# Token halves at the ends of the feed-forwards: a tail of five tiles, and the next norm's transposes among other products

## What is computed

```python
x = x + (gelu(gate) * (h @ ffn_w_val)) @ ffn_w_down      # block 1, gate = causal conv of h @ ffn_w_gate
x = rmsnorm(x, norm_final)
for l in range(2):                                       # block 2
    x = layer_norm(alpha * x + 0.5 * swiglu(x, w_gu[l,0], w_down[l,0]), ...)
    x = layer_norm(alpha * x + token_mixers(x), ...)
    x = layer_norm(alpha * x + 0.5 * swiglu(x, w_gu[l,1], w_down[l,1]), ...)
```

## Time and profile before

| | |
|---|---|
| median of three runs | 1370.58 us |
| profiled execution, span from first to last instruction | 1368.9 us |
| TensorE busy | 1331.6 us, 97% |
| VectorE busy | 893.2 us, 65% |
| ScalarE busy | 755.2 us, 55% |
| chain that ended last | TensorE 77%, VectorE 12%, ScalarE 8% |
| DMA | 228.9 MB, mean 167 GB/s |

### The profile page before, as it was taken

The page is one execution under the profiler, slowest core; times in us unless marked ns, Lnnn a source line. Parts: engine busy times, 40 slices in busy tenths (PEclk is TensorE's granted clock), DMA queues, the critical chain, the costliest instruction groups (busy, mean ns, idle before and its releaser), DMA issues.

```text
span 1368.9 us, 20197 instructions
## 1 busy us (share of the span) xinstructions
PE 1331.6 (97%) x8028; PEld 1154.7 (84%) x8047; DVE 893.2 (65%) x1329; ACT 755.2 (55%) x1216; POOL 80.5 (6%) x132
## 2 busy tenths in 40 slices
PE   7999899999999999999999999999999999999997
PEld 6888788887888889887888888888889887888886
DVE  5887776766665667465766656656667465766565
ACT  6776655555555554655555554655554655555553
POOL 2121000000000002400000000000001500000000
PEclk9999999999999999999999999999999999999999
DMA  7334576664766654333576665766655333476660
GB/s 234 124 124 145 157 223 197 197 209 128 244 187 186 194 163 143 93 124 94 153 241 194 185 186 151 224 195 191 192 155 147 107 124 93 128 235 196 196 196 34
DMA packets 294959, 228.90 MB, mean 167 GB/s; under 512 B 13248, under 2 KB 271443, under 8 KB 294867
## 3 DMA queue, kind: packets, MB, share of 16 engines
q1 hardware_dynamic: 294850, 227.62, 55.0%
q10 hardware_dynamic: 16, 0.00, 0.0%
HBM read 226.54 MB, written 1.05 MB: 166 GB/s over the span
## 4 chain that ended last, share of the span: by engine, by line
PE 77%; DVE 12%; ACT 8%; issue 2%; DMA 2%; POOL 0%; SPq 0%; DVEq 0%; ACTq 0%
PE bank L885 21%; PE bank L802 12%; PE bank L803 12%; PE bank L804 12%; PE bank L888 11%; DVE lo_gu L1763 4%; ACT hi_gu L1369 3%; PE bank L1272 3%; DVE lo_dn L1768 2%; PE bank L1241 2%; DVE conv L1947 1%; DMA st_dn<-in_ffn_w_down 1%; PE bank L1252 1%; ACT conv L1485 1%; DVE xT L1778 1%
## 5 line engine op out<-in xcount | busy, mean ns | idle before, releaser
L885 PE MATMUL bank<-xT,hi_gu 128*128 128x512 f32 x1616 | 404.1, 392 | 2.3 <-DVE lo_gu L1763 2.1
L1763 DVE TENSOR_TENSOR lo_gu<-st_gu,hi_gu 128x2048 fp32r<-128x2048 f32 (+1 forms) x145 | 322.7, 2229 | 101.0 <-ACT hi_gu L1369 101.0
L885 PEld LDWEIGHTS bank<-xT,hi_gu 128*128 128x128 f32 x1616 | 296.7, 189 | 60.7 <-DVE lo_gu L1763 3.3
L1369 ACT ACTIVATE hi_gu<-st_gu 128x2048 fp32r<-128x2048 f32 (+2 forms) x146 | 269.9, 1854 | 0.9 <-DMA st_gu<-in_w_in 0.8
L888 PEld LDWEIGHTS bank<-xT,lo_gu 128*128 128x128 f32 x1616 | 220.8, 191 | 15.9
L888 PE MATMUL bank<-xT,lo_gu 128*128 128x256 f32 x1616 | 225.5, 282 | 0.0
L802 PE MATMUL bank<-hi_dn,actTh 128*128 128x512 f32 x436 | 172.3, 395 | 3.2 <-DVE actTl L1959 3.2
L803 PE MATMUL bank<-lo_dn,actTh 128*128 128x512 f32 x436 | 170.7, 392 | 0.0
L804 PE MATMUL bank<-hi_dn,actTl 128*128 128x512 f32 x436 | 169.9, 390 | 0.0
L1950 DVE TENSOR_TENSOR act<-act,bank 128x256 f32<-128x256 f32 x101 | 42.5, 421 | 177.7 <-ACT act L1492 177.7
L1376 ACT ACTIVATE hi_dn<-st_dn 128x1024 fp32r<-128x1024 f32 x109 | 114.1, 1056 | 62.3 <-DMA st_dn<-in_ffn_w_down 62.3
(11 more groups left out here) (294 smaller groups left out, 1781.5 us busy)
## 6 DMA issues: line engine op xcount, KB each, us to landing
st_gu<-in_ffn_w_gu SPq DMA_DIRECT2D x176, 512.0 KB, 5.1
st_dn<-in_ffn_w_down SPq DMA_DIRECT2D x109, 512.0 KB, 6.3
st_gu<-in_w_in SPq DMA_DIRECT2D x23, 1024.0 KB, 5.4
st_gu<-in_w_out SPq DMA_DIRECT2D x24, 512.0 KB, 4.2
st_gu<-in_ffn_w_gate SPq DMA_DIRECT2D x21, 512.0 KB, 4.2
st_gu<-in_ffn_w_val SPq DMA_DIRECT2D x21, 512.0 KB, 5.6
st_gu<-in_w_in SPq DMA_DIRECT2D x10, 512.0 KB, 4.1
gb<-in_ln_g SPq DMA_DIRECT2D x6, 512.0 KB, 7.0
```

The lines of the kernel that those rows point to most:

```text
L885: pe.matmul(b[:, :], hv[:, w, k, :], xT[:, k, :, :].rearrange("p a b -> p (a b)"), start=k == 0, stop=k == KD - 1, skip_group_check=True)
L1369: i = act.activation(high, staged, ACT.Copy)
L1763: i = dve.tensor_tensor(low, staged, high.bitcast(F32), ALU.subtract)
```

## The change

`TAIL` and `RING` go from 4 to 5: the last five tiles' downs go by token halves, and there is a fifth buffer for down weights, laid over `gbo`. `turn` of the next norm's first token half moves from the start of the next stage to before the last down of the second half (not at norms 4, 7 and 8). `turn` of the second half moves, in feed-forwards 1 to 4, from between the tiles into the first half's products of the second tile (before step k = 6 of 8 in f = 1, 3, before k = 4 in f = 2, 4), and the four fills behind it go. At the start of f = 1, 3 and of the projections two fills stay of four. In VectorE's `norm` the low copies of the first half, and before them at norms 2 and 5 the low weights of the next feed-forward's second tile, come before the second half's add.

```diff
-TAIL = 4
-RING = 4
+TAIL = 5
+RING = 5
...
-            def gate_up_tokens(f, j, m, event=None, turned=None):
+            def gate_up_tokens(f, j, m, event=None, turned=None, norm_turned=None):
...
+                    if norm_turned is not None and k == (KD - 2 if f % 2 else KD // 2):
+                        turn(x, norm_turned, 1)
                     i = mm3(o, (xTh[:, k, ts], xTl[:, k, ts]), (hv[:, :, k, :], lv[:, :, k, :]), k == 0, k == KD - 1)
...
-            def ffn(f, i, src):
+            def ffn(f, i, src, turned_next=None):
+
                 tail = range(FFN_TILES[f] - TAIL, FFN_TILES[f])
-                turn(src, i, 0)
-
                 idle = 6 + tile_no(f, 0) % 2
-                fill(idle, 4)
+                if f % 2:
+                    fill(idle, 2)
+                else:
+                    turn(src, i, 0)
+                    fill(idle, 4)
...
                     gate_up_tokens(f, 0, 0, i)
-                    gate_up_tokens(f, 1, 0)
+                    gate_up_tokens(f, 1, 0, norm_turned=i)
                     fill(idle, 1)
-                    turn(src, i, 1)
-                    fill(idle, 4)
                     gate_up_tokens(f, 0, 1, i)
...
                 for m in range(M):
                     for j in tail:
+                        if m == 1 and j == tail[-1] and turned_next is not None:
+                            turn(x, turned_next, 0)
                         down(f, j, m)
...
-                turn(x, i, 0)
-                fill(7, 4)
+                fill(7, 2)
                 token_half(c, 0, bank[0][:, 0:WCOLS], i)
...
+                    if m == 1 and i != LAST:
+                        if i in (2, 5):
+                            weights_low(CHUNK_NO["ffn", i // 2 + i % 2, 1])
+                        turned_low(i, 0)
                     for h in range(2):
                         add(i, m, h)
                     centre(i, m)
-                    if m == 1 and i != LAST:
-                        turned_low(i, 0)
-                        if i in (2, 5):
-                            weights_low(CHUNK_NO["ffn", i // 2 + i % 2, 1])
                     normalize(i, m)
```

More of the change, by code:

```diff
@@ L268, in program @@
         hi_out2, lo_out2 = over("hi_out2", KD * WCOLS, at_proj), over("lo_out2", KD * WCOLS, at_proj + 4 * KD * WCOLS)
-        hi_dn = [over(f"hi_dn{i}", D, (at_down, at_proj)[i // 2] + 4 * D * (i % 2)) for i in range(RING)]
-        lo_dn = [over(f"lo_dn{i}", D, (at_down, at_proj)[i // 2] + 4 * (KD * WCOLS + D * (i % 2))) for i in range(RING)]
         act32 = sb("act32", [P, 2, S])
@@ L288, in program @@
         rs = sb("rs", [P, M])
+        at_gbo = -(-nc.sbuf_base // 32) * 32
         gbo = sb("gbo", [P, M, D])
+        hi_dn = [over(f"hi_dn{i}", D, (at_down, at_proj)[i // 2] + 4 * D * (i % 2)) for i in range(4)] + [over("hi_dn4", D, at_gbo)]
+        lo_dn = [over(f"lo_dn{i}", D, (at_down, at_proj)[i // 2] + 4 * (KD * WCOLS + D * (i % 2))) for i in range(4)] + [over("lo_dn4", D, at_gbo + 4 * D)]
         ones = sb("ones", [P, 1])
@@ L1107, in tensor_program @@
                     out_part(m, h, 1)
-            ffn(0, 1, n)
+            ffn(0, 1, n, 2)
             def first_projections(l):
@@ L1354, in tensor_program @@
             for l in range(LAYERS):
-                ffn(1 + 2 * l, 2 + 3 * l, x)
+                ffn(1 + 2 * l, 2 + 3 * l, x, 3 + 3 * l)
                 mixers(l)
-                ffn(2 + 2 * l, 4 + 3 * l, x)
+                ffn(2 + 2 * l, 4 + 3 * l, x, 5 + 3 * l if l + 1 < LAYERS else None)
         def scalar_program(act):
```

## The result

The changed kernel takes **1375.7 us** (median of seven runs, 1372.83 to 1377.91) against 1370.58 (seven runs, 1369.91 to 1373.05). The ratio is 1.0035, 95% interval 1.0025 to 1.0044: 5 us slower, where the forecast was no visible change. The profiled execution took 1376.42 us, its span is 1374.9, 6.0 above the one before. Lines on TensorE are one higher than before (L885 is L886), on VectorE and ScalarE five (L1763 is L1768).

A forecast was written before the change was run, and what follows sets the result against it. TensorE, busy 97% of the span, was taken as the bound, except at feed-forward 0's end (vector/scalar loop). Terms 0, +0.3, -0.3, -0.9, +0.6, -0.3, +0.2 gave -0.4 us: 1370.2 us from 1370.58, range 1366.8 to 1372.8.

The forecast's parts named there:

- tail waits: Last gate-up of feed-forwards 1 to 4 waits for its low weights: 0.3, 0.9, 0.55 and 0.2 us.
- joint 2 to 3: From feed-forward 2 into 3: first product no earlier or later, second transposes inside the second tile win 0.9 us.
- 7.4 us chain: Feed-forward ends: vector/scalar loop steps from ScalarE's copy of the down weights to the low weights add up to 7.4 us.
- A deeper ring at no cost: Fifth down-weight buffer over gbo: loosens ScalarE's wait for old downs, which shows in no row; 0 us.
- if the clock stays up: End of feed-forward 0: gate-up 20 waits 1.1 us, keeps full pace, ends at 317.6; last down +1.1 us.
- +2.8 from 319.3: End of feed-forward 0, the other case: gate-up 20 slow again, ends at 319.3; last down 2.8 us later.
- rival B: Tail waits lower the clock for the last gate-ups of feed-forwards 1 to 4: 1377.6 us, 1374 in two; chance 7%.
- Norm 3: Into the first projections: product 0.8 us earlier, but second transposes wait for the late second half; +0.3 us left.
- norm 6: Into the second projections: product earlier, second transposes wait; +0.6 us with the 0.55 us tail wait before it.
- rival A: Handovers and second tiles gain without new waits: 6.9 us, 1363.7 us, half of it 1367; chance 15%.
- no gain and no loss: Into feed-forward 3: first half normed 845.1, low weights and copy until 848.2, so first product at 848.25 as before.
- own case: Whole kernel: no visible change, 1370.2 us, chance 77%; terms' ends -1.2 to +1.3 us, range 1368.5 to 1372.

The follow-up runs named there:

- early down loads: Changed kernel with the last two tiles' loads ordered gate-up pair, down weights, pair, down weights, instead of two pairs then two downs: 1372.7 us, ratio 1.0013.
- The second execution: The changed kernel as it is, run and profiled again beside the other kernels on one chip: 1375.2 us, ratio 1.0036.
- the one that wins: Kernel before with only the second transposes moved inside the second tile: 1369.4 us; with k = 6 in all four feed-forwards 1368.5 us.

## Why the prediction was wrong

The profile came out 6.4 us above the forecast of its change (+6.0 against -0.4). Of these 3.2 are two falls of the clock in the mixers, which the sum did not have; 1.9 are the tail waits beyond their forecast; 0.9 the loops of 1 to 4; 0.5 the joint 2 to 3 beside its wait. The smaller terms add 0.5, and 0.55 had been won by the last tiles of feed-forward 0's loop, before anything that the change moves. In the medians, which are 5.5 us above the forecast, the lower clock has a smaller part (1 to 2 us by the estimate above), and the tail waits are the largest step that an experiment shows.

**Tail waits, feed-forwards 1 to 4: mis-sized.** Forecast 0.3 + 0.9 + 0.55 + 0.2 = 1.95 us; measured from gate-up 20 to 21, beyond 5.59: 0.87 + 0.95 + 1.77 + 0.25 = 3.8. The mechanism and the 7.4 us chain were right. Two things were not. I took the moments at which the down weights had landed from one execution and let them stand, though the change itself may shift the traffic around them: ScalarE's wait at the end of feed-forward 3 went from 1.52 to 2.69 us. And the same kernel has other ones in its next execution: at the end of feed-forward 4 it was 1.11 us in one and 2.04 in the other, and TensorE's wait behind it 0.09 and 0.95. Second, a wait costs more than its bracket, 0.16 us more by the matmuls that no longer overlap, so that the 0.09 us ones lengthen the step by 0.25; and 0.1 more in the gate-up behind it, which the sum of 3.8 leaves out. The early down loads show it: the waits fall to 0.09, and the time by 3.0 us. That is more than the 1.9 that was mis-sized, since it takes away most of the 1.95 that was forecast too.

**A deeper ring at no cost: failed.** I set the fifth buffer at 0. In every kernel with `RING` 5, the one with `TAIL` 4 among them, each fifth tile of the loops is 0.05 us longer and the next 0.02 to 0.03; in none with `RING` 4. Timeline of TensorE in the changed kernel, the 12 downs of tile 24 in buffer five: 371.62 to 374.41 is 2.79 us; the next tile's, 380.00 to 382.74, 2.74.

```profile
371.62 0.39 PE L803 MATMUL bank<-hi_dn,actTh 128*128 128x512 f32 x1
...
374.41 0.39 PE L886 MATMUL bank<-xT,hi_gu 128*128 128x512 f32 x1
...
380.00 0.40 PE L803 MATMUL bank<-hi_dn,actTh 128*128 128x512 f32 x1
...
382.74 0.39 PE L886 MATMUL bank<-xT,hi_gu 128*128 128x512 f32 x1
```

Over the loops of 1 to 4 that is the +0.9 us of the table (0.23 + 0.29 + 0.15 + 0.20). Why these matmuls are slower is open: no run has the fifth buffer at another place.

**Feed-forward 0, "if the clock stays up": right in the profile after, unsafe as a choice.** The case "+2.8 from 319.3" happened in two of the six profiles with five tiles there (the two without the moves), and once the fall came at gate-up 20 with the moves on top (+0.8). The sum took the good case at full weight. One of the last two gate-ups of feed-forward 0 was slow in each of the six profiles with five tiles, never both: in three it was 19, behind 2.08 to 2.16 us; in the other three 19 kept its pace behind 2.16 to 2.18, and 20 was slow behind 2.47 or 2.48. None was slow behind the waits of 0.09 to 1.61 us in 1 to 4. So rival B did not happen, though its 1374 lay near the result.

The case that "TensorE: Matmul & The Clock Gate" of the Trainium skill describes in its section "HAM oscillation — how this bites in real kernels" is one of DMA waits of 3 to 5 us, each longer than any wait here. The prediction put it to waits of 0.2 to 2.3 us, which the section does not do. The traces agree with neither reading: half clock came behind 2.1 us, but not every time.

**The norms and the second tiles: right but for one overlap.** Norm 3 cost 1.08 us and 0.87 of it is the tail wait; norm 6 1.96, of which 1.77: 0.2 us beside the wait, forecast 0 to 0.05. The product came first (520.84 against 520.55 forecast) and the wait went ahead of the second transposes, which rival A excluded. Feed-forwards 2 and 4 started 0.4 us better each (forecast 0.3), with idles of 0.52 and 0.51. Feed-forward 1 starts unchanged (forecast 0). The joint 2 to 3 won 0.3 instead of 0.9. There the forecast let the tail wait of 0.9 us vanish, because VectorE's own chain was to hold the first product back: "no gain and no loss". But VectorE had to wait 0.99 us for the delayed downs of the first half (the row at 842.51), and the first product came 0.5 us later against the tiles before it. With the wait gone the joint won 1.0. The end of feed-forward 4 cost 0.5 (forecast 0.2), 0.36 of it the step and the gate-up behind its wait of 0.09 us.

**The mixers: missing.** Two falls of the clock; the mixers with the first products behind them took 1.6 us more each (from 0.77 late behind norm 3 to 2.39 late at the start of feed-forward 2). They are why the span is 6.0 longer and not some 3. The second execution had none, and its span was as long: it was 1.1 us late at the start of feed-forward 0 already, lost 0.8 where gate-up 20 was slow, and waited longer at the end of feed-forward 4. The range written for the own case, 1368.5 to 1372, is wider than its terms (-1.2 to +1.3 from 1370.2 is 1369.0 to 1371.5), and the result lies outside both. The prediction's last sentence, that a wait ahead of these second transposes decides between it and rival A, held.

What stays open: by medians the changed kernel with early down loads is 2.1 us above the kernel before. Its profile is 3.4 us longer. Of these 1.2 were lost by tile 17 of feed-forward 0, which is the execution and not the kernel: at this tile six profiles of kernels with the same instructions up to there lie from 0.86 ahead to 1.29 behind. Another 1.6 are a fall in the mixers. The remaining 0.6 belong to the kernel (the loops and the four last gate-ups, +1.8, less what the transposes inside and norm 5 win). By the clock of its runs the lower clock costs it about 1 us more than the kernel before (4.7 against 3.7 on average); whether the change brings that about is not shown.

## What to carry to other kernels

Where work is moved from between two products to behind them, the products' next input must be ready earlier by as much: look up which wait already stands behind a DMA on the engine that makes it, and put the load first in its queue; this was worth 3.0 us here. A time at which a DMA lands can be another one in the next execution of the same kernel, so bound it by the longest wait of its kind and not by the one in the same place. And test the parts alone: the one that wins (2.2 to 2.9 us at k = 6) was hidden under those that lose.

## What was not expected of the hardware

- The clock fell or stayed behind equal waits. In feed-forward 0 2.13 us (before) and 2.08 (after) brought half clock, 2.30 (only the transposes inside) did not. The timeline of TensorE there, and the windows behind it:

```profile
312.26 0.50 PE L885 MATMUL bank<-xT,hi_gu 128*128 128x512 f32 x1 [2.30 <-DVE lo_gu L1763]
```

```profile
314.00:316.00 2.00, 2.00 (x14) 1.82 (x13) 0.97 (x3) 0.89 (x2) 0.00 (x0) 1.00 1.11 327
```

- In the mixers, where no single wait of TensorE is above 1.01 us, it fell in 11 of 28 cases, each time within 0.8 us behind the same wait of 0.87 us, and nowhere else in the group.
- Eight transposes that had to wait take 1.32 and 1.25 us in the rows at 525.48 and 856.15, and 1.03 at 518.33 straight behind matmuls. They are hardly slower one by one: the second four start when VectorE has written the second normed column half (in the changed kernel it ends at 526.09, and they start at 526.15).
- A single issue of a 512 KB down load has a row of 1.9 us on the queue that issues it (the kernel with early down loads, below), two of them one of 3.07 (above).

```profile
1004.60 1.94 SPq L589 DMA_DIRECT2D st_dn<-in_ffn_w_down  x1
```
